# Nine quarters of the normalised activations made on TensorE during the routing, and a first expert block that starts on half of its tokens

## The reference

```python
def layer_norm(x, g, b):
    mu = jnp.mean(xf, -1, keepdims=True)
    var = jnp.mean(jnp.square(xf - mu), -1, keepdims=True)
    return (xf - mu) * lax.rsqrt(var + LN_EPS) * g + b

x = layer_norm(ALPHA * x + mix, ln1_g, ln1_b)            # called x1 here
g_idx = top_1(x @ w_group + b_group)                     # one of 4 groups
e_idx = top_2((x @ w_router + b_router)[group g_idx])    # two of its 4 experts
gate  = softmax weights of the two * softmax weight of the group
h = silu(x @ w_gate[e]) * (x @ w_up[e])                  # 16 experts, 2048 -> 512
y = sum over e of gate[e] * (h @ w_down[e])
out = layer_norm(ALPHA * x + y, ln2_g, ln2_b)
```

## Time and profile before

| | us |
|---|---|
| median of three runs | 1537.92 (1537.3 to 1543.0) |
| the profiled execution, its time | 1536.54 |
| its span in the profile | 1534.7 |
| PE busy | 1468.1 (96% of the span) |
| DVE busy | 988.5 (64%) |
| ACT busy | 748.4 (49%) |

### The profile page before, as it was taken

The page is one execution under the profiler, slowest core; times in us unless marked ns, Lnnn a source line. Parts: engine busy times, 40 slices in busy tenths (PEclk is TensorE's granted clock), DMA queues, the critical chain, the costliest instruction groups (busy, mean ns, idle before and its releaser), DMA issues.

```text
span 1534.7 us, 24078 instructions
## 1 busy us (share of the span) xinstructions
PE 1468.1 (96%) x9374; PEld 1293.9 (84%) x9374; DVE 988.5 (64%) x1222; ACT 748.4 (49%) x868; POOL 183.5 (12%) x92
## 2 busy tenths in 40 slices
PE   8999999999999989999999599999999999999994
PEld 7998898889999989999999347888888888888782
DVE  4234525436778687821222747888888888888886
ACT  4234333334433332411110137777777877777774
POOL 0000000000000000134331001221111122122110
PEclk9999999999999999999999699999999999999997
DMA  7321231132222132525333599999999999999997
GB/s 272 107 82 56 88 109 56 56 90 91 90 78 96 51 106 71 164 101 210 119 103 110 187 363 385 384 375 387 387 375 383 387 380 393 388 385 398 365 286 226
DMA packets 89173, 335.36 MB, mean 219 GB/s; under 512 B 11776, under 2 KB 18480, under 8 KB 60124
## 3 DMA queue, kind: packets, MB, share of 16 engines
q1 hardware_dynamic: 84058, 315.54, 55.4%
q0 software_dynamic: 5040, 18.74, 4.8%
HBM read 313.56 MB, written 40.73 MB: 231 GB/s over the span
## 4 chain that ended last, share of the span: by engine, by line
PE 83%; DVE 9%; DMA 6%; ACT 1%; issue 1%; SPq 0%; DVEq 0%; ACTq 0%; POOLq 0%
PE BANK L1647 13%; PE BANK L1648 13%; PE BANK L1649 12%; PE BANK L1993 6%; PE BANK L1995 6%; PE BANK L1994 6%; DMA RAWB<-in_w_up 4%; PE BANK L2032 4%; PE BANK L2030 4%; PE BANK L2031 4%; PE BANK L1977 2%; PE BANK L1709 2%; PE BANK L1732 2%; PE BANK L1788 1%; PE BANK L1665 1%
## 5 line engine op out<-in xcount | busy, mean ns | idle before, releaser
L1647 PE MATMUL BANK<-XH,HI 128*128 128x260 f32 x1746 | 506.6, 290 | 0.8 <-issue 0.5
L1520 DVE TENSOR_TENSOR LOB<-RAWB,HIB 128x2048 fp32r<-128x2048 f32 x196 | 448.9, 2293 | 87.2 <-ACT HIB L961 86.7
L1648 PE MATMUL BANK<-XL,HI 128*128 128x260 f32 x1746 | 496.3, 284 | 0.0
L1649 PE MATMUL BANK<-XH,LO 128*128 128x260 f32 x1746 | 495.5, 284 | 0.0
L961 ACT ACTIVATE HIB<-RAWB 128x2048 fp32r<-128x2048 f32 x196 | 376.3, 1920 | 117.9 <-PE BANK L1995 71.7
L1647 PEld LDWEIGHTS BANK<-XH,HI 128*128 128x128 f32 x1746 | 332.1, 190 | 17.2 <-issue 16.5
L1648 PEld LDWEIGHTS BANK<-XL,HI 128*128 128x128 f32 x1746 | 332.1, 190 | 0.0
L1649 PEld LDWEIGHTS BANK<-XH,LO 128*128 128x128 f32 x1746 | 332.0, 190 | 0.0
L1993 PE MATMUL BANK<-HIB,XGH 128*128 128x512 f32 x512 | 202.1, 395 | 7.5 <-DVE LOB L1520 3.4
L1995 PE MATMUL BANK<-LOB,XGH 128*128 128x512 f32 x512 | 200.3, 391 | 0.0
L1994 PE MATMUL BANK<-HIB,XGL 128*128 128x512 f32 x512 | 200.0, 391 | 0.0
(11 more groups left out here) (346 smaller groups left out, 1585.4 us busy)
## 6 DMA issues: line engine op xcount, KB each, us to landing
RAWB<-in_w_down SPq DMA_DIRECT2D x68, 1024.0 KB, 10.8
RAWB<-in_w_gate SPq DMA_DIRECT2D x67, 1024.0 KB, 9.5
RAWB<-in_w_up SPq DMA_DIRECT2D x67, 1024.0 KB, 9.8
RAW<-in_w_in SPq DMA_DIRECT2D x39, 1024.0 KB, 5.0
RAW<-in_w_out SPq DMA_DIRECT2D x16, 1024.0 KB, 5.4
Y<-in_xT SPq DMA_DIRECT2D x8, 520.0 KB, 9.1
RT<-in_xT SPq DMA_DIRECT2D x16, 260.0 KB, 5.2
x_rows<-R SPq DMA_DIRECT2D x5, 832.0 KB
```

What stands on the lines that cost most here:

```text
L1520: dve.tensor_tensor(LOB[:, s, :], RAWB[:, r, :], HIB[:, s, :].bitcast(F32), ALU.subtract).then_inc(b_lo[s], 1)
L1647: pe.matmul(bank, hw[:, c, :], h, start=(c == 0), stop=False)
L1648: pe.matmul(bank, hw[:, c, :], l, start=False, stop=False)
L1649: ins = pe.matmul(bank, lw[:, c, :], h, start=False, stop=(c == KC - 1))
```

## The change

Nine quarters (`WHOLE`: groups 0, 1 and 2, columns 0 to 1535) are made whole on PE. A product with a diagonal matrix `DIAG` that holds 1/sd, in fp32, and the shift product on top of it in the same PSUM bank give x1, and ACT copies it into R. Two of the nine stand before the rank products, six between rank and table products, one behind the first block's own shift products. DVE keeps eleven quarters (`SHIFTED`), four early and seven during the first block.

For that, the correction's inputs come earlier. ACT writes two columns of C5 and builds DIAG right after 1/sd is known, DVE makes the third column before `first(...)`, and PE turns C5 before it waits for the one-hots. ACT's first Exp, and the table load that belongs to it, move behind the copies of L5. Rank products now go to bank 7.

SP stores groups 0 to 2 of x1 as soon as their parts are there, and y_set(0) right behind them; the other four y_set stand one load earlier than before. The first block's products begin when the first of the four token groups is copied; groups 2 and 3 are turned behind its second and third weight tile. The seven remaining shift products stand one by one between products, from the second tile on.

```diff
-            act.wait_ge(r_e, 1)
-            act.activation(G4[1][:, :, :], G4[1][:, :, :], ACT.Exp).then_inc(r_x, 1)
+            act.wait_ge(s_var, 2)
+            act.activation(C5[:, :, 0:1], MV[0:TT, :, 3:4], ACT.Copy)
+            act.activation(C5[:, :, 2:3], MV[0:TT, :, 3:4], ACT.Copy).then_inc(s_sd, 1)
+            for i in range(NT):
+                ins = act.activation(DIAG[:, i, :], IDENT[0:TT, 0:TT], ACT.Copy, scale=MV[0:TT, i, 2:3])
+            ins.then_inc(s_sd, 1)
...
+            def whole_copy(k):
+                i, c = WHOLE[k]
+                act.wait_ge(s_t5, 3 + k if k < 8 else 4 + k)
+                act.wait_ge(s_x1w, 16 * 3)
+                act.activation(R[:, i, 512 * c:512 * c + 512], BANK[0:TT, whole_bank(k), :], ACT.Copy).then_inc(s_sd, 1)
...
             def x1_out(i):
-                q = 4 * i + 4
-                sp.wait_ge(s_x1, q if q <= EARLY_X1 else q + 4)
+                if i < 3:
+                    sp.wait_ge(s_sd, 3 * i + 6)
+                sp.wait_ge(s_x1, (1, 2, 3, 11, 15)[i])
...
+            y_set(0)
...
+            def whole_scaled(k):
+                i, c = WHOLE[k]
+                if k == 2:
                     pe.wait_ge(s_rcp, 5 * NT)
+                elif 4 <= k < 8:
+                    pe.wait_ge(s_sd, k)
+                pe.matmul(BANK[0:TT, whole_bank(k), :], DIAG[:, i, :], R[:, i, 512 * c:512 * c + 512], start=True, stop=False)
+
+            def whole_shifted(k):
+                shift(BANK[0:TT, whole_bank(k), :], *WHOLE[k], False).then_inc(s_t5, 1)
...
             pe.wait_ge(s_l5, 1)
             shift_turned(4, 0).then_inc(s_t5, 1)
-            shift_quarter(0)
-            shift_quarter(1)
+            pe.wait_ge(s_sd, 3)
+            pe.wait_ge(s_rcp, 3 * NT)
+            for k in range(2):
+                whole_scaled(k)
+            pe.wait_ge(s_l5, 2)
+            for k in range(2):
+                whole_shifted(k)
+
+            pe.wait_ge(r_hot, 1)
...
             ins.then_inc(r_rank, 1)
+            for k in range(2, 8):
+                whole_scaled(k)
+                whole_shifted(k)
             pe.wait_ge(r_tab, 1)
...
             pe.wait_ge(s_l5, 3)
+            pe.wait_ge(s_sd, 11)
             for g in range(4):
                 own = GB5[:, :].rearrange("r (a k) -> r k a", k=KC)[:, 4 * g:4 * g + 4, :]
                 pe.matmul(BANK[:, Q0_BANK[g], :], L50[:, :], own, start=True, stop=True).then_inc(s_q, 1)
-            for q in range(2, EARLY_X1):
+            whole_scaled(8)
+            whole_shifted(8)
+            for q in range(EARLY_X1):
                 shift_quarter(q)
...
             def first_gate_up():
-                pe.wait_ge(b_xh, 4)
                 q = EARLY_X1
                 for i in range(8):
+                    pe.wait_ge(b_xh, i // 2 + 1)
...
-                        if q < 4 * NT:
+                        if i >= 1 and q < len(SHIFTED):
                             shift_quarter(q)
-                            shift_quarter(q + 1)
-                            q += 2
+                            q += 1
+                    if i in (1, 2):
+                        tokens(i + 1, 0)
...
-            for g in range(4):
+            for g in range(2):
                 tokens(g, 0)
             first_gate_up()
```

More of the change, by code:

```diff
@@ L438, in q_bank, with whole_bank @@
             return 6 + q % 2 if q < EARLY_X1 else (6, 7, 4, 5)[q % 4]
+        WHOLE = [(k // 3, k % 3) for k in range(EARLY_WHOLE)]
+        SHIFTED = [(i, 3) for i in range(4)] + [(3, c) for c in range(3)] + [(4, c) for c in range(4)]
+        def whole_bank(k):
+            return (0, 1, 4, 5)[k % 4] if k < 8 else 3
         def last_bank(k, n):
@@ L946, in _ @@
             act.activation(MV[0:TT, :, 2:3], MV[0:TT, :, 1:2], ACT.Sqrt, bias=EPS_LN[0:TT, :]).then_inc(s_sd, 1)
-            act.wait_ge(r_e, 1)
-            act.activation(G4[1][:, :, :], G4[1][:, :, :], ACT.Exp).then_inc(r_x, 1)
-            act.wait_ge(r_e, 2)
-            act.activation(DIF[:, :], DIF[:, :], ACT.Exp).then_inc(r_x, 1)
+            act.wait_ge(s_var, 2)
[4 more added lines that the diff above has]
+            ins.then_inc(s_sd, 1)
             act.wait_ge(s_t5, 1)
@@ L954, in _ @@
             act.activation(L5[:, 4 * TT:T], BANK[0:5, 7, 0:TT], ACT.Copy).then_inc(s_l5, 1)
+            def whole_copy(k):
[3 more added lines that the diff above has]
+                act.activation(R[:, i, 512 * c:512 * c + 512], BANK[0:TT, whole_bank(k), :], ACT.Copy).then_inc(s_sd, 1)
+            act.wait_ge(r_e, 1)
+            act.activation(G4[1][:, :, :], G4[1][:, :, :], ACT.Exp).then_inc(r_x, 1)
+            for k in range(2):
+                whole_copy(k)
+            act.wait_ge(r_e, 2)
+            act.activation(DIF[:, :], DIF[:, :], ACT.Exp).then_inc(r_x, 1)
+            for k in range(2, 8):
+                whole_copy(k)
             def bhi(i, m0, j):
@@ L1543, in _ @@
                 first_tokens(g)
-            for q in range(EARLY_X1, 4 * NT):
+            for q in range(EARLY_X1, len(SHIFTED)):
                 x1_quarter(q)
@@ L1914, in shift_turned, with shift @@
                 return pe.transpose(BANK[0:5, 7, col:col + TT], C5[:, i, :].bitcast(F32), IDENT[0:TT, 0:TT])
+            def shift(bank, i, c, start):
+                return pe.matmul(bank, L5[:, i * TT:i * TT + TT], GB5[:, 512 * c:512 * c + 512], start=start, stop=True)
             def shift_quarter(q):
[L1917 to L1937 removed]
+                i, c = SHIFTED[q]
+                if 2 <= q < EARLY_X1 + 2:
+                    pe.wait_ge(s_x1, q - 1)
+                elif q >= EARLY_X1 + 2:
+                    pe.wait_ge(s_x1, q + 1)
+                shift(BANK[0:TT, q_bank(q), :], i, c, True).then_inc(s_q, 1)
+            def whole_scaled(k):
+                i, c = WHOLE[k]
+                if k == 2:
+                    pe.wait_ge(s_rcp, 5 * NT)
+                elif 4 <= k < 8:
[3 more added lines that the diff above has]
+                shift(BANK[0:TT, whole_bank(k), :], *WHOLE[k], False).then_inc(s_t5, 1)
+            pe.wait_ge(s_rc, 176)
             pe.wait_ge(s_c5, 1)
@@ L1943, in _ @@
             shift_turned(4, 0).then_inc(s_t5, 1)
-            shift_quarter(0)
-            shift_quarter(1)
+            pe.wait_ge(s_sd, 3)
[3 more added lines that the diff above has]
+            pe.wait_ge(s_l5, 2)
+            for k in range(2):
+                whole_shifted(k)
+            pe.wait_ge(r_hot, 1)
+            hot = RK[:, :, :].rearrange("p i e -> p (i e)")
+            tri, ones = TRIR[:, 0, :], TRIR[:, 1, :]
+            pe.matmul(BANK[0:TT, 7, 0:80], tri, hot, start=True, stop=False)
+            for s in range(1, NT):
+                pe.matmul(BANK[0:TT, 7, 16 * s:80], ones, hot[:, 0:80 - 16 * s], start=False, stop=(s == NT - 1))
+            for i in range(NT):
+                ins = pe.matmul(BANK[0:TT, 7, 96:112], ones, RK[:, i, :], start=(i == 0), stop=(i == NT - 1))
+            ins.then_inc(r_rank, 1)
+            for k in range(2, 8):
+                whole_scaled(k)
+                whole_shifted(k)
             pe.wait_ge(r_tab, 1)
```

58 lines of the change are left out of this document (24 added, 34 removed).

## The result

The changed kernel took 1547.84 us in the median of seven runs (1544.07 to 1553.81), the kernel before 1538.5 (1535.31 to 1543.0) beside it: a ratio of 1.006, 95% interval 1.0043 to 1.0077. It is slower by 0.6%. The profiled execution took 1545.3 us, its span 1543.5, which is 8.8 more than before.

The account below looks back on a forecast made before the run. PE and DMA are full in the steady loop, so only its start can move: tile 7 starts 3.6 us earlier and 1.5 us of lower clock goes, 5.1 in sum. Forecast 1532.8 us; 8 in 10 between 1529 and 1540.

Parts of the forecast that it names:

- six pairs between rank and table: Routing on PE: six pairs at full clock, 1.49 us each, 8.9 us, so table products start 2.7 us later.
- Rank products: Routing: two pairs ahead of them, mostly at 1.2 GHz, delay them by 1.8 us; +2.3 at half clock, +0 at full.
- Table products: Routing: start at 862.5 against 859.78 us, +2.7; +8.9 with half clock throughout.
- PE arrives warm: Ten table products, 2.37 us cold, take half with the clock up: -1.1 us.
- First DVE quarter: Behind the ninth pair and first early shift product, DVE's quarter starts at 867.6 instead of 865.26 us, +2.4.
- `first_tokens`: Behind four DVE quarters costing as before, it starts at 871.3 instead of 868.88 us.
- First block: First product 3.3 us behind `first_tokens`, -0.3; PE's work -0.7, half-speed products +0.9; block ends at about 909.2, as now.
- Transfers and block 1: 2.0 MB less queued, tile 7 lands 4.2 us earlier; its start -3.6, no clock fall behind it -1.5.
- tile 7's landing is not a matter of bytes: Rival, chance 0.13: block 1's second tile needs its time whatever is queued; everything +1.1 us late, stall stays, 1539.
- half clock through all nine pairs: Rival, chance 0.13: table +8.9, first product +9.2, tile 7 +5.1, less 1.5; slower by 3.6 us, 1541.5.
- slower by over 0.5%: Measured time above 1545.6 us; chance 0.05, taking the half clock and something more.
- the evidence of 875 to 888: Trace of the kernel before: PE kept clock 1.00 there with products and shift products mixed; cited against the half-clock rival.

Follow-up runs that it names:

- four, four, two, two: Changed kernel, only reordered between rank and table: four diagonal products, their four shift products, then two and two; 1542.92 us, ratio 1.002 (on 128 rows 1540.24 us, 0.9996).
- 128-row version: Changed kernel with all nine diagonal products padded to 128 rows and 128 columns, added ones zero; 1541.85 us against 1538.82, ratio 1.0032.
- the rearranged first block: Kernel before with only its first block begun on half of the tokens; 1541.37 us against 1539.58, ratio 1.0004.
- first-part-alone version: Changed kernel with the nine quarters, but all token groups turned ahead of the first block as before; 1554.52 us, one run.
- 128x128 product: Changed kernel with its first eight diagonal products replaced by fp32 products of 128x128 on 128x512; 1543.1 us, one run.
- six-quarter version: Changed kernel with six whole quarters on 128 rows: one pair ahead of rank, five between rank and table; 1554.51 us against 1538.82, ratio 1.0109.
- eight quarters: Changed kernel with eight whole quarters on 128 rows, two products back to back ahead of rank, five alternating pairs behind; 1535.99 us against 1539.65, ratio 0.9979.

## Why the prediction was wrong

The failed step is the one for the **six pairs between rank and table**: "I take the full clock, because PE then has had work since 847.5 without a gap". PE had that work, without a gap from 846.6 to behind the table products, and the clock stayed at 0.50 for it. A pair cost 2.65 us instead of 1.49, six 15.9 instead of 8.9. With the same instructions in the order four, four, two, two the six cost 10.6. Step by step, with shifts measured from the square root:

- **Rank products**: forecast +1.8, measured +2.2 (9.26 against 7.09). Right, near the bound given for the half clock.
- **Table products**: forecast +2.7, upper bound +8.9, measured +9.9. The bound took 2.4 for a pair at half clock, from 1.71 for a product and some 0.7 behind it (and wrote 14.6 for 6 x 2.4, which is 14.4). The 1.49 at full clock held 0.2 us for the change from product to shift product (1.06 against 0.86), and the bound left that out: product to shift product took 1.97 (855.72 to 857.69), shift product to product 0.68.
- **PE arrives warm**, -1.1: it did not come; the ten table products took 2.38 us. In the versions with the clock up they took 1.32, so the size was right.
- **First DVE quarter**: forecast +2.4, measured at 877.77, +13.2. To the 9.9 come 3.3 from the table products on: the ninth pair and the first early shift product at half clock.
- **`first_tokens`** behind it, forecast unchanged, took 5.11 us instead of 3.62: 2.11 idle, of which the chain shows 1.29 as DVE's sequencer reading a register (`value_load`, which stands between the quarters and `first_tokens` in both kernels). Before, DVE was idle for 0.63 there; why the reading didn't show then is open.
- **First block**: first product 3.10 us behind `first_tokens`, forecast 3.3; right. Five passes ran at 0.86 before the clock came back, +2.1 instead of +0.9.
- **Transfers and block 1**: forecast that less is queued. From the second load to the first down tile it took 951.04 - 903.47 = 47.6 us, before 942.19 - 890.16 = 52.0: 4.4 shorter, of the 6.2 that the forecast's numbers give (891.3 to 937.1). The second tile took 9.9 us from issue to landing instead of 11.7, and from its issue to tile 7's landing it took 39.5 instead of 42.9 (forecast 37.6). PE's wait fell from 2.00 to 0.25 us and the clock held, so block 1 took 3.6 us less from gate/up to the first down tile, where the forecast's numbers give 3.5. The mechanism was right, and the rival that tile 7's landing is not a matter of bytes is out. The forecast had the gather landed by the end of the first block; PE still waited 1.69 us for it (1.48 before). None of this could repay 13.1 us of a late block 1.

The sum as measured: first product +11.8, block 1's gate/up +13.1, less 3.6 in block 1: +9.5; the square root stood 0.7 earlier, so the span is 8.8 longer.

The rival **half clock through all nine pairs** (0.13) is what happened. It gave 1541.5, 3.6 slower, and this was 8.8: its first product was put 2.6 us too early, its first block had nothing for the clock, where 1.3 more were lost, and it credited 5.6 us back against 3.6. More than that block 1 did not have to give: the stall of 2.00 and the 1.5 us of lower clock behind it are all but gone in the changed kernel. It gave "slower by over 0.5%" 0.05 in all, as needing the half clock and something more. The half clock alone explains most: the 128-row version returns 6.6 of 9.5 us at the end and 7.4 at the first down tile, and its order four, four, two, two all of them (690.7 against 701.4, before 691.9).

Of the rivals in the experiments, the rearranged first block is out (1.0004 alone). That PE's work in front of the table costs at any clock is not shown for any part of the 9.5: the 2.9 that the 128-row version kept include a ninth pair and a start of the first block at 0.50, and they are within the 3 us by which single profiles differ. But no gain is shown either. With nine quarters and the clock up through the pairs the median is that of the kernel before (0.9996), not 5.1 us below it as forecast, and the first tokens stay 4.1 us late. So the forecast's gain is not there even where the clock is up for the six pairs; the ninth pair, at the half clock there too, is one part of that.

The prediction had put the Trainium skill beside this rival ("TensorE: Matmul & The Clock Gate", A second HAM failure mode: PE idle for moments between groups, cycling PSUM banks, keeps changing its clock) and set the evidence of 875 to 888 against it. That page's cause is not at work here: between 855 and 868 PE has no idle moment in the windows, and its clock doesn't change but stays at 0.50. And the row from 875 to 888 was a misleading neighbour, because the clock was already up when the mixture of shapes began. One shift product behind each product doesn't take it away then either (1.00 from 892.56 to 903.13 in the changed kernel). What the row couldn't show is whether the clock rises within such a mixture: begun at 0.50 it stayed down in all six pairs here, and for 20 us in the first block of the first-part-alone version.

What it is about the alternation is narrowed, not settled. Shown: without the 5-row products it rises (104 rows); with four products in a row it rises (104 rows); in strict alternation it doesn't at 104 rows, whatever zeros or columns; at 128 rows it was up in the profiled run with two large products in a row ahead of the rank products, was not with one, and was lost again in a third. Put together: in no profile did the clock rise within strict alternation. Where it was up as the alternation began, it held through six pairs twice (128x128 product, 128 rows) and in the first block of the changed kernel and of the six-quarter version, and was lost after one pair with eight quarters. Why is open. Whether it was the same in each unprofiled run is open, and so is the spread of the change's own runs (four at 1544.07 to 1547.84, three at 1552.65 to 1553.81). A first block that stays at the half clock, 6.7 us in the first-part-alone profile, would be of that size; no profile shows it for the change.

## What to carry to other kernels

Busy is not warm: price every piece of TensorE work that is put on a critical chain at both clock levels, and if the sum has another sign at the lower one, give that case a real chance, unless a row shows the clock rise within this very sequence of shapes: a row in which it was already up doesn't. If tiny products must go with large ones, put several of each in a row; here it took four PSUM banks, which the pairs used anyway. And look first at what stands in front of a chain's next consumer: work "in the shadow" of a wait of 4.59 us was 15.9 us long.

## What the runs showed of the hardware

- PE busy for 13.00 of 13 us (855 to 868) with fp32 products of 104x104 on 104x512 and 5x104 on 5x512 in turn was granted 0.50 throughout. The same instructions in the order four, four, two, two had 0.88 of the clock in the window of 860 to 865.
- Such a mixture, with 128x128 on 128x512, kept a clock that was up as it began: 1.00 for 10.57 us (892.56 to 903.13) in the changed kernel. Begun at 0.50 it stayed there for 20 us in the first-part-alone version.
- The clock can be lost without a gap: 0.97 in one window of 2 us, 0.50 in the next, PE busy 2.00 of 2 in both.
- Whether the matrix is diagonal or full made no difference to it: the same 0.50 with both.
- At 1.2 GHz two fp32 passes of 104 rows with the change to a 5-row product behind them cost 1.97 us; eight in a row cost 0.88 each (7.00). Ten table products cost 2.38 at 1.2 GHz and 1.32 behind a stretch at 2.4.
